# A Fourier stage folded by symmetry, and half of an output product moved between the heads of an mLSTM stage

## What is computed

```python
proj = h @ w_in
q, k, v, o, fz, gates = jnp.split(proj, np.cumsum(IN_SPLITS)[:-1].tolist(), axis=-1)
y_mlstm = _mlstm_group(q, k, v, o, gates, b_gate, mlstm_norm_w)
y_fourier = _fourier_group(fz)
mix = jnp.concatenate([y_mlstm, y_fourier], axis=-1) @ w_out
x = _ln_affine(ALPHA * x + (1 + g1) * mix, ln1_g, ln1_b)
```

## Time and profile before

| | us |
|---|---|
| median of three runs | 3781.57 (3771.51 to 3787.52) |
| the profiled execution's own time | 3770.92 |
| its span, first to last instruction | 3769.1 |
| TensorE busy | 3586.4 (95%) |
| VectorE busy | 1824.0 (48%) |
| ScalarE busy | 1216.4 (32%) |
| GpSimd busy | 519.0 (14%) |
| mean granted clock of TensorE | 0.97 |

### The profile page before, as it was taken

The page is one execution under the profiler, slowest core; times in us unless marked ns, Lnnn a source line. Parts: engine busy times, 40 slices in busy tenths (PEclk is TensorE's granted clock), DMA queues, the critical chain, the costliest instruction groups (busy, mean ns, idle before and its releaser), DMA issues. The chain is left out here.

```text
span 3769.1 us, 41502 instructions
## 1 busy us (share of the span) xinstructions
PE 3586.4 (95%) x16012; PEld 2865.7 (76%) x16012; DVE 1824.0 (48%) x2293; ACT 1216.4 (32%) x1746; POOL 519.0 (14%) x287
## 2 busy tenths in 40 slices
PE   8979999999998999879999999999977899999998
PEld 6757888888786777648888888888766678888886
DVE  7986423232266666655322233555357874323235
ACT  4335411111244444454311112444432353212123
POOL 0016100000061000035000000451001540000004
PEclk9989999999999999989999999999977999999999
DMA  2102213122132111102222132232221223111113
GB/s 100 36 31 79 95 61 100 50 89 72 47 102 59 40 45 50 45 17 90 84 76 85 44 117 90 93 96 95 69 73 40 78 73 95 56 45 50 45 56 101
DMA packets 75999, 261.17 MB, mean 69 GB/s; under 512 B 10224, under 2 KB 10608, under 8 KB 75888
## 3 DMA queue, kind: packets, MB, share of 16 engines
q1 hardware_dynamic: 75888, 259.69, 21.6%
HBM read 246.54 MB, written 4.72 MB: 67 GB/s over the span
## 5 line engine op out<-in xcount | busy, mean ns | idle before, releaser
L197 PE MATMUL ps<-xh,whi 128*128 128x512 f32 x2816 | 982.4, 394 | 45.6 <-DVE wlo L180 19.0
L197 PE MATMUL ps<-xl,whi 128*128 128x512 f32 x2816 | 974.5, 391 | 0.0
L197 PE MATMUL ps<-xh,wlo 128*128 128x512 f32 x2816 | 974.3, 391 | 0.0
L180 DVE TENSOR_TENSOR wlo<-stage,whi 128x1024 fp32r<-128x1024 f32 x366 | 524.9, 1434 | 514.6 <-ACT whi L174 513.5
L174 ACT ACTIVATE whi<-stage 128x1024 fp32r<-128x1024 f32 x366 | 386.5, 1056 | 1080.4 <-PE ps L197 1032.7
L197 PEld LDWEIGHTS ps<-xh,whi 128*128 128x128 f32 x2816 | 532.3, 189 | 164.6 <-issue 30.6
L197 PEld LDWEIGHTS ps<-xh,wlo 128*128 128x128 f32 x2816 | 532.0, 189 | 111.4
L197 PEld LDWEIGHTS ps<-xl,whi 128*128 128x128 f32 x2816 | 532.5, 189 | 109.8
L197 PE MATMUL ps<-hh,whi 128*128 128x512 f32 x1216 | 422.6, 396 | 6.0 <-ACT lam_t L2050 3.9
L197 PE MATMUL ps<-hl,whi 128*128 128x512 f32 x1216 | 421.5, 395 | 0.0
L197 PE MATMUL ps<-hh,wlo 128*128 128x512 f32 x1216 | 421.5, 395 | 0.0
(11 more groups left out here) (371 smaller groups left out, 3906.0 us busy)
## 6 DMA issues: line engine op xcount, KB each, us to landing
stage<-in_w_ff SPq DMA_DIRECT2D x88, 512.0 KB, 3.6
stage<-in_w_gate SPq DMA_DIRECT2D x59, 512.0 KB, 3.3
stage<-in_w_up SPq DMA_DIRECT2D x59, 512.0 KB, 3.3
stage<-in_w_in SPq DMA_DIRECT2D x50, 512.0 KB, 3.2
ada<-in_w_ada SPq DMA_DIRECT2D x48, 512.0 KB, 3.4
stage<-in_w_qkv SPq DMA_DIRECT2D x43, 512.0 KB, 3.4
stage<-in_w_down SPq DMA_DIRECT2D x48, 448.0 KB, 3.4
stage<-in_w_out SPq DMA_DIRECT2D x32, 512.0 KB, 3.2
```

The lines of the kernel that those rows point to most:

```text
L180: dve.tensor_tensor(wlo[slot][:], stage[slot][:], whi[slot][:].bitcast(F32), ALU.subtract).then_inc(w_split, 1)
L197: done = pe.matmul(acc[:, h * HALF:(h + 1) * HALF], wt[slot][:, w], xt[:, b, h * HALF:(h + 1) * HALF], start=b == 0 and wt is whi and xt i ...
```

## The change

**Folding.** VectorE folds the Fourier part while the input product runs: tokens n and n + 512 are added and subtracted, and the sums once more at 256 (`fold`, in place in `zt`). Output positions that are multiples of 4, and those that are 2 more than one, then need only 256 folded tokens each, odd positions 512. The token transform has four blocks as before, but with 2, 2, 4 and 4 token blocks instead of 8 each; its weights are three units instead of eight. The channel table keeps 65 cosines and 65 sines of 128 each (the others are mirrors), so `channels(n)` has 130 columns instead of 256, a matmul of the token transform 260 instead of 512, and VectorE writes straight and mirrored channels in four operations for each block instead of two.

**The output product.** Its part "first 512 tokens x the 512 Fourier features" is calculated in the mLSTM block: eight `early_unit`s of 12 matmuls on TensorE, one before and one after parts of each head's work, into the half of a PSUM bank pair that the scores gave up (the scores of a head are made in two halves). For each there is a load on SyncE's queue (`early_load`, 256 KB), a split by ScalarE (`early_hi`) and GpSimd (`early_lo`), an eviction with the gate by ScalarE (`early_out`) and an addition to x by GpSimd (`early_add`). `o2a` then has 12 matmuls per unit and units of half the width. The scaling of x by `ALPHA_2` goes from `gated_half` to eight GpSimd operations of 128 x 1024 during the input product. The normalisation of a head's output goes from VectorE to ScalarE (eight operations with scale and bias; VectorE's `scale_of` prepares them).

The order on the engines changes too: ScalarE does the exponentials of heads 0 and 1 before the first two evictions, and those of head h + 1 (h = 1, 2) after `early_out(2h + 2)`.

The core of the diff (left out are layouts of tables and tiles, the two-part forms of `scores` and `weighted_scores`, and the helpers named above):

```diff
-        def __init__(self, n, src, halves=(0, 1)):
+        def __init__(self, n, src, halves=(0, 1), width=D):
...
-        act.activation(whi[slot][:], stage[slot][:], ACT.Copy).then_inc(w_hi, 1)
+        act.activation(whi[slot][:, wide(g, k)], stage[slot][:, wide(g, k)], ACT.Copy).then_inc(w_hi, 1)
...
-    plan["dft"] = Product(NT, blocks(io["dft"]))
-    split_product("out2", DB, blocks(io["w_out2"]))
+    plan["dft"] = Product(3, blocks(io["dft"]))
+    plan["out2a"] = Product(DB, groups(io["w_out2"], 0, MH), (0,), MH * P)
+    plan["out2b"] = Product(DB, blocks(io["w_out2"]), (1,))
...
+    def fold(dve, b):
+
+        z, quarter = zt[:, b, :], HALF // 2
+        dve.wait_ge(acc_free, i2b.base + Z_AT + b + 3)
...
+        dve.tensor_tensor(folded, z[:, 0:HALF], z[:, HALF:S], ALU.add).then_inc(z_fold, 1)
+        dve.tensor_tensor(z[:, HALF:S], z[:, 0:HALF], z[:, HALF:S], ALU.subtract).then_inc(z_fold, 1)
+        dve.wait_ge(z_fold, 4 * b + 2)
+        dve.tensor_tensor(z[:, 0:quarter], folded[:, 0:quarter], folded[:, quarter:HALF], ALU.add).then_inc(z_fold, 1)
+        dve.tensor_tensor(z[:, quarter:HALF], folded[:, 0:quarter], folded[:, quarter:HALF], ALU.subtract).then_inc(z_fold, 1)
...
                 gates_dve(dve, u)
+                if u >= Z_AT + 2 and u - Z_AT - 2 < 4:
+                    fold(dve, u - Z_AT - 2)
...
                 fn1.sums_pool(pool, h)
+            for b in range(DB):
+                pool.tensor_scalar(x[:, b, :], x[:, b, :], ALPHA_2, None, ALU.mult).then_inc(scaled, 1)
...
-                    done = pe.matmul(ps[n % 2][:, g * 2 * P:(g + 1) * 2 * P], zt[:, g, n * P:(n + 1) * P], cs, start=True, stop=True)
+                    at = (g // 2) * HALF + (g % 2) * 2 * PART
+                    done = pe.matmul(ps[n % 2][:, at:at + 2 * PART], zt[:, g, n * P:(n + 1) * P], cs, start=True, stop=True)
...
             for t in range(NT // 2):
-                pe.wait_ge(acc_free, gdft.base + 2 * t)
+                u = dft_unit(t)
+                slot, kbs = (gdft.base + u) % 2, 2 if t < 2 else 4
+                pe.wait_ge(w_split, gdft.base + u + 3)
+                if t >= 2:
+                    pe.wait_ge(y_out, Y0 + 4 * (t - 1))
...
                 for k in range(2):
-                    for b in range(DB):
+                    for b in range(kbs):
...
+    def early_unit(pe, u):
+
+        hi, lo = early_split(u)
+        pe.wait_ge(e_lo, E_N + u + 1)
+        if u:
+            pe.wait_ge(e_out, E_N + u)
...
+        for b in range(MH):
+            w = slice(b * P, (b + 1) * P)
+            for wt, xt in ((hi, xh), (hi, xl), (lo, xh)):
+                done = pe.matmul(EARLY_BANK, wt[:, w], xt[:, MH + b, 0:HALF], start=b == 0 and wt is hi and xt is xh,
+                                 stop=b == MH - 1 and wt is lo)
+        done.then_inc(e_mm, 1)
...
             for h in range(2):
+                early_load(sp, h)
                 for e in range(2):
                     stabiliser(h, e)
...
-            scores(0)
+            scores(0, 0)
             updates(0)
+            early_unit(pe, 0)
+            scores(0, 1)
+            early_unit(pe, 1)
             for h in range(MH):
                 numerators(h, 0)
                 if h + 1 < MH:
+                    scores(h + 1, 0)
+                    early_unit(pe, 2 * h + 2)
                     updates(h + 1)
-                    scores(h + 1)
+                    scores(h + 1, 1)
+                    early_unit(pe, 2 * h + 3)
                     numerators(h, 1)
...
+            for u in range(DB):
+                early_add(pool, u)
+                if u + 2 < DB:
+                    early_lo(pool, u + 2)
+                if u == 3:
+                    select(2)
+                if u == 5:
+                    select(3)
...
             for b in range(MH):
                 act.activation(xh[:, MH + b, :], yf[:, b, :], ACT.Copy).then_inc(yf_hi, 1)
+                if b < 2:
+                    early_hi(act, b)
             weights(0)
+            weights(1)
+            for u in range(2):
+                early_out(act, u)
+                early_hi(act, u + 2)
             for h in range(MH):
                 if h:
                     deviation(h - 1)
-                if h >= 2:
-                    high(h - 2)
-                if h + 1 < MH:
-                    weights(h + 1)
+                    normalise(h - 1)
+                for u in (2 * h + 2, 2 * h + 3):
+                    if u < DB:
+                        early_out(act, u)
+                        if u + 2 < DB:
+                            early_hi(act, u + 2)
+                    if u == 2 * h + 2:
+                        if h >= 2:
+                            high(h - 2)
+                        if h and h + 1 < MH:
+                            weights(h + 1)
...
                 if h + 1 < MH:
                     state_queries(h + 1, 0)
+                    weighted_scores(h + 1, 0)
                     states(h + 1)
-                    weighted_scores(h + 1)
+                    weighted_scores(h + 1, 1)
...
-        dve.tensor_scalar(blk, blk, ALPHA_2, 0.0, ALU.mult, ALU.add).then_inc(scaled, 1)
-        dve.wait_ge(scaled, DB * h + u + 1)
+        dve.wait_ge(*((scaled, DB) if h else (e_add, E_N + u + 1)))
...
-            product_pe(pe, o2a, DB, xh, xl, ready)
+            product_pe(pe, o2a, MH, xh, xl, ready)
```

More of the change, by code:

```diff
@@ L145, in program, with wide @@
         count = 0
[L147 to L148 removed]
+        def __init__(self, n, src, halves=(0, 1), width=D):
+            self.base, self.n, self.src, self.halves, self.width = Product.count, n, src, halves, width
             Product.count += n
+    def wide(g, k):
+        return slice(0, g.width if k < g.n else D)
     def load(sp, g, i, k):
@@ L2356, in _, with dft_unit, dft_tokens @@
                     dve.memset(v1[:, :, :, MDV:MDV + 1], 1.0).then_inc(ones_col, 1)
+    FIRST_K = (0, 2, 1, HALF // 2 + 1)
+    def dft_unit(t):
+        return max(t - 1, 0)
+    def dft_tokens(t, mirrored):
+        step, first = (4 if t < 2 else 2), FIRST_K[t]
+        if not mirrored:
+            return slice(first, first + step * P, step)
+        skip = 1 if t == 0 else 0
+        return slice(S - first - step * skip, S - first - step * P, -step)
     with nc.Block(no_gpsimd_drain=True) as block:
@@ L2504, in _, with scores @@
         def _(pe):
-            def scores(h):
+            def scores(h, k):
                 hb = half_rows(h)
-                if h:
-                    pe.wait_ge(m_pt, 2 * h)
+                if h or k:
+                    pe.wait_ge(m_pt, 4 * h + 2 * k)
                 if h >= 3:
                     pe.wait_ge(m_y, h - 2)
-                for c in range(NT):
-                    t = slice(c * P, (c + 1) * P)
-                    done = pe.matmul(ps[0][:, t], kt[hb, h // 2, t], qt[hb, h // 2, t], start=True, stop=True)
+                for c in range(NT // 2):
+                    t = slice(k * HALF + c * P, k * HALF + (c + 1) * P)
+                    done = pe.matmul(ps[0][:, c * P:(c + 1) * P], kt[hb, h // 2, t], qt[hb, h // 2, t], start=True, stop=True)
                 done.then_inc(m_sc, 1)
```

205 lines of the change are left out of this document (144 added, 61 removed).

## The result

The changed kernel took 3743.2 us (median of five runs, 3735.8 to 3748.7) beside 3781.6 for the kernel before: a ratio of **0.9902, 95% interval 0.9881 to 0.9924**, 38 us less. The forecast was 3770, within 0.5% of no change; the time lies 0.2 us inside the lower end of the range. The likeliest case did not come: the change is faster by 1%.

The account below looks back on a forecast made before the run. Dense stages were taken as bound mainly by TensorE, the mLSTM stage by each head's longest ring of hand-overs. Channel -3, token -30, output product -21 and -3.5, mLSTM +46 sum to -11.5 us: 3770 against 3781.6, range 3743 to 3793.

Parts of the forecast that it names:

- The likeliest case: Whole kernel: gains in the dense stages nearly paid back by ScalarE's order in the mLSTM stage; 3770 us, chance 0.58.
- The first total of the output product: Output product, first half: TensorE totals GpSimd's sums some 31 us after the stage begins, before 51.7; -21 us.
- The second half: Output product, second half: VectorE is in the chain and loses eight scalings; -3.5 us, between 0 and -6.
- the ring: mLSTM heads 1 and 2: chain of hand-overs from numerators to numerators, 41 us against 25.0 before, +16 each.
- the exponentials of head 0 and of head 1, four times 4.78: mLSTM stage, beginning: ScalarE does these to 30.3 us, and only then evicts the first burst.
- exponentials 9.56: mLSTM heads 1 and 2: ScalarE's exponentials for the next head, 9.56 us within a sum of 35 to 47.
- the start: mLSTM stage up to head 0's numerators: TensorE waits for ScalarE's first eviction; 36.0 us against 21.6, +14.
- the two transforms: Channel transform -3 us (-6 to +5) and token transform -30 us (-34 to -24), from less TensorE work.
- 129 slow columns as a bound for 130: Channel transform: if 130 columns behave like 129, 0.24 us a record, nothing gained or up to 5 us lost.
- Rival 2: mLSTM stage: TensorE stays at 2.4 GHz between bursts, stage grows by 35 us; 3756 us, chance 0.30.
- Rivals 3 and 4: 3: bursts fit TensorE's idle mLSTM time, 3724 us, chance 0.04; 4: TensorE stays at 1.2 GHz, 3820 us, chance 0.08.
- nearly paid back: Whole kernel: the mLSTM stage's +46 us nearly cancels the dense stages' gains, leaving -11.5 us; chance 0.58.

## Why the prediction was right and wrong

**Right, by its steps.** The first total of the output product came at 30.3 us behind its start (31 forecast; before it came at 51.1, as the window of 51.7 reaches past it). GpSimd's two sums per block took 1.79 and 1.56 us in the mean over both halves, 3.35 the pair, against the 3.2 taken from the earlier trace rows. But they are hardly the bound: TensorE, busy for 29.6 of the 30.3 us, waits 0.24 us for them, not one or two.

```profile
L380 POOL TENSOR_TENSOR sum_c<-sum_c,x 128x512 f32<-128x512 f32 x12 | 21.5, 1794 | 5.2 <-DVE x L2940 5.2
L390 POOL TENSOR_TENSOR sum_c<-sum_c,sq_c 128x512 f32<-128x512 f32 x11 | 17.1, 1559 | 1.0 <-ACT sq_c L370 1.0
...
2927.09 1.92 PE L401 MATMUL ps<-share,sum_c 128*128 128x2 f32 x16 [0.24 <-POOL sum_c L390]
```

The second half gave 2.9 (3.5). Folds and scaling cost nothing that shows: the stretch that holds them is 1011.4 us before and 1010.8 to 1011.9 in all runs after, though a scaling of GpSimd takes 2.8 us there. The order of the ring is as I described it, shown by the run that moved the exponentials out of it (-11.6 us in the stage, 12 in the whole). The table load cost 1.28 us with nothing around it once more (normalisation to 2795.62, load from 2795.64, exponentials from 2796.93 above), where the Trainium skill ("ScalarE: Activation LUTs", section "What ACT_TABLE_LOAD costs") adds a drain of 1.38; no row here shows it.

**Wrong: the step "the exponentials of head 0 and of head 1, four times 4.78", and "exponentials 9.56" in the ring.** The group of 16 that I had read the earlier trace rows is a whole head in both directions; I took it for one direction. A count would have told: `weights` issues 2 x 8 for a head, 64 in the stage. This put 9.6 us too much into the start and 4.8 into each ring. With the right number the sum's own terms give 14 - 9.6 = 4.4 for the start (measured 6.5) and 16 - 4.8 = 11 for a ring (measured 15.6 and 9.2), so 46 - 19.2 = 27 for the stage (measured 30.3) and 3751 for the time. The prediction had named its own test: a stage below 165 us would refute the ring. It took 164.9 and 163.5, so the ring as it was summed is refuted, if narrowly, while its order stands.

**Wrong in its cause though near in size: the start.** I forecast TensorE waiting for ScalarE's first eviction. In the trace ScalarE had nothing to do by then. The start was late because its copies stood behind two loads. Behind that, hidden until it was taken away, VectorE stood for a broadcast: state queries stand ahead of the states in the changed kernel, and I had given that no price. Only with both gone did TensorE wait for the eviction as forecast, and with that gone too the numerators came at 21.6 to 23.2, where they were before (21.6). The first load took 5.3 us from the stage's start, not the 2.7 worked out from a load that had no broadcasts beside it.

**Mis-sized: the two transforms**, -43.4 instead of -33, each beyond the end of its range (-8.5 beside -6, -34.9 beside -34). I let 1.2 GHz into the token transform's first two blocks and kept 129 slow columns as a bound for 130; both were TensorE's clock, not its shape. These 10 us and the 16 of the mLSTM stage went the same way, and that brought the time to the range's edge.

**The rivals.** Rival 2 came nearest in the time (3756, ring 35), but not by its reason: the bursts did not hold 2.4 GHz through the gaps of head 1, whose ring opened at 0.52, and with the exponentials counted right its ring would be 30, where the one that opened at 1.00 took 33.9. Rivals 3 and 4 are out. That the gains were "nearly paid back" holds for the bursts alone, as the run without them shows: 23.7 us gained, 22 to 29 paid.

## What to carry to other kernels

Work that is moved into another stage's idle time costs what it does to the order of each engine's queue, not its length on the engine that was idle: price every wait that it puts ahead of an instruction somebody needs, and then try the orders, one at a time and in pairs, since where two limits lie side by side lifting one alone may leave the ring as long as it was. Before a group of instructions is multiplied, count the group against the loop that issues it. And measure a mixed change without its second half: here all of the gain was in the first, until the second was put in another order.

## What the runs showed of the hardware

In a stage with gaps of some microseconds TensorE's clock differed between two executions of one program, by 7.0 us in 134; differences of that size need timed runs or the granted clock beside them. Other groups ran at a clock that followed the order of work in every profile. With 12 matmuls of 512 columns put into a wait of 2.3 us, the numerators behind it took 6.1 us in all three profiles, and without them 10.3 to 10.6 in all eleven others. Where two bursts had been taken out of head 2's ring, its backward numerators took 11.0 us in both profiles, and 6.2 to 6.3 in the twelve others. The missing bursts alone are not the cause: three of those twelve are of kernels that never had any, and TensorE does not wait there. In the two slow ones it waits 3.0 and 7.3 us just ahead, with only eight score matmuls between the wait and the numerators; in the changed kernel it waits 6.8 us at the same place, with a burst behind it, and the numerators take 6.2. The transforms next to it, which TensorE fills, took 33.0 to 33.5 us in all thirteen profiles that have them folded.
